# Both directions of a chunked RWKV-7 scan on all four quarters of TensorE

## The reference

```python
h = rms_norm(x, norm_mix);  p = h @ w_in                      # 1024 -> 4832 columns
z = centred_shift(p[..., :RWKV_COLS], mu_prev, mu_next)
y_a = rwkv7_branch(z, ...) @ w_o_rwkv                         # bidirectional recurrence
y_b = conformer_conv_branch(u, ...) @ w_o_conv
x = x + (g_a * y_a + g_b * y_b) @ w_out
x = x + expert_choice_ffn(rms_norm(x, norm_ffn), ...)         # 16 experts
```

```python
def step(S, inp):
    r_t, w_t, k_t, v_t, a_t, b_t = inp
    sa = jnp.einsum('bhij,bhj->bhi', S, a_t)
    S = (S * w_t[:, :, None, :] + sa[..., :, None] * b_t[..., None, :]
         + v_t[..., :, None] * k_t[..., None, :])
    return S, jnp.einsum('bhij,bhj->bhi', S, r_t)
```

## Time and profile before

| | us |
|---|---|
| median of 3 runs | 2510.17 |
| lowest and highest | 2505.96, 2513.14 |
| the profiled execution | 2512.39 |
| its span, first to last instruction | 2510.6 |

### The profile page before, as it was taken

One profiled execution on the slowest core, in us unless ns is written; L12 is line 12 of the kernel. 1 busy time (PEld: TensorE's weight loads), 2 busy tenths in 40 slices (PEclk: granted clock), 3 DMA queues, 4 the chain that ended last, 5 costly groups with the idle time before them and its releaser, 6 DMA issues. The chain is left out here.

```text
span 2510.6 us, 50080 instructions
## 1 busy us (share of the span) xinstructions
PE 2330.4 (93%) x19504; PEld 2038.1 (81%) x19504; DVE 1825.2 (73%) x2480; ACT 1207.5 (48%) x1748; POOL 704.6 (28%) x715
## 2 busy tenths in 40 slices
PE   6899999999986999997989996699999999999997
PEld 4788888888876899986767674699999999999996
DVE  5547888988865576665767677677777777777777
ACT  6355454445522334433335332566555666666656
POOL 2234242433412444455454534001111111101011
PEclk9999999999997999998999998799999999999998
DMA  4335353442537767763647352777777777777777
GB/s 151 85 97 162 86 160 117 135 151 85 173 112 226 210 184 190 193 163 94 235 133 252 105 201 101 301 252 251 268 257 245 237 254 259 248 254 259 263 255 239
DMA packets 294772, 479.74 MB, mean 191 GB/s; under 512 B 142224, under 2 KB 209952, under 8 KB 266832
## 3 DMA queue, kind: packets, MB, share of 16 engines
q1 hardware_dynamic: 275552, 412.52, 50.4%
q0 software_dynamic: 7760, 27.08, 4.9%
q10 hardware_dynamic: 11296, 37.82, 4.6%
HBM read 363.51 MB, written 110.69 MB: 189 GB/s over the span
## 5 line engine op out<-in xcount | busy, mean ns | idle before, releaser
L2749 PE MATMUL bank<-e_xt,e_w_high 128*128 128x384 f32 x1792 | 525.2, 357 | 2.3 <-DVE e_xt L2917 2.3
L2904 DVE TENSOR_TENSOR e_w_low<-e_w,e_w_high 128x2048 fp32r<-128x2048 f32 x192 | 435.9, 2284 | 69.8 <-ACT e_w_high L2805 69.8
L2750 PE MATMUL bank<-e_xt,e_w_low 128*128 128x192 f32 x1792 | 449.3, 251 | 0.0
L2805 ACT ACTIVATE e_w_high<-e_w 128x2048 fp32r<-128x2048 f32 x192 | 366.1, 1908 | 108.0 <-PE bank L2771 79.2
L2750 PEld LDWEIGHTS bank<-e_xt,e_w_low 128*128 128x128 f32 x1792 | 342.5, 191 | 0.6
L2749 PEld LDWEIGHTS bank<-e_xt,e_w_high 128*128 128x128 f32 x1792 | 338.3, 189 | 3.9 <-issue 2.7
L462 PE MATMUL bank<-h_high,w_high 128*128 128x512 f32 x864 | 257.9, 407 | 1.5 <-DVE work L872 1.5
L855 DVE SCALAR_TENSOR_TENSOR work<-work,vec 128x1551 f32<-128x1551 f32 x116 | 243.8, 2102 | 2.4
L465 PE MATMUL bank<-h_low,w_high 128*128 128x512 f32 x864 | 244.8, 391 | 0.0
L468 PE MATMUL bank<-h_high,w_low 128*128 128x512 f32 x864 | 243.7, 390 | 0.0
L2683 POOL DMA_INDIRECT xacc_dram<-e_y,e_put x30 | 47.3, 1576 | 652.0 <-DVE e_y L2939 647.5
(11 more groups left out here) (356 smaller groups left out, 5164.6 us busy)
## 6 DMA issues: line engine op xcount, KB each, us to landing
e_w<-in_ew SPq DMA_DIRECT2D x192, 1024.0 KB, 5.5
features_dram<-work SPq DMA_DIRECT2D x48, 512.0 KB, 3.3
fe<-features_dram SPq DMA_DIRECT2D x24, 1024.0 KB, 8.3
x_w<-in_w_mix SPq DMA_DIRECT2D x48, 512.0 KB, 4.1
w<-in_w_in ACTq DMA_DIRECT2D x35, 512.0 KB, 3.6
ba_tok_dram<-work SPq DMA_DIRECT2D x96, 128.0 KB, 2.2
gates_dram<-work ACTq DMA_DIRECT2D x16, 768.0 KB, 4.6
all<-ba_tok_dram SPq DMA_DIRECT2D x96, 128.0 KB, 3.3
```

The lines of the kernel that those rows point to most:

```text
L2749: nc.tensor.matmul(*wide, start=(k == 0), stop=False)
L2750: nc.tensor.matmul(*narrow, start=False, stop=False)
L2805: nc.scalar.activation(w_high[n % RING][:], w[n % RING][:], ACT.Copy).then_inc(w_high_done, 1)
L2904: tt(w_low[n % RING][:], w[n % RING][:], w_high[n % RING][:].bitcast(F32), ALU.subtract)\
```

## The change

Direction 1 keeps its inputs where they were, but its 64x64 products go to the other half of the partitions: `HALF[d]` gives the output half, `ROWS` for direction 0 and `ROWS[::-1]` for direction 1. So where the two directions' matmuls alternate, four in a row fall on four different quarters. `level_n`, `level_x` and `solve` become one section for both directions; `products` is cut into `products_wide` (128 columns) and `products_narrow` (64), each for both directions, and `products_c` alternates too.

What comes out exchanged is put back: DVE adds the identity for direction 1 in two instructions of 64 partitions, ACT copies `XX` and `GH` of direction 1 in halves, and the copies of level 0 are cut by side for both directions. For direction 1 state and token rows change places (`STATE`, `TOKEN`) and so does the order of B, A, M in `ALL`, with the store of `ba_tok` in `project` to match. The level masks write the blocks that they need, in two instructions, into buffers cleared at the start. `ALL` has six buffers instead of five.

The orders of PE, DVE and ACT are written anew: narrow products behind level_x(0), wide ones behind level_n(1), products_c before level_x(1), and state(1, i-1) moves from the end of `body(i)` to `body(i+1)` behind its first level_n. SP's and POOL's orders stay; SP's store of G waits for the wide mask alone.

```diff
-        ALL = many("all", [P, HP, 5, CH], RING)
-        B_, A_, M_, G_, RB_ = range(5)
+        ALL = many("all", [P, HP, 5, CH], RING_ALL)
+        B_, A_, M_, G_, RB_ = (0, 2), (1, 1), (2, 0), (3, 3), (4, 4)
+        STATE, TOKEN = ROWS, ROWS[::-1]
+        HALF = [ROWS, ROWS[::-1]]
...
+                    x = XX if n else X0
                     for hp in L4:
-                        for r in ROWS:
-                            mm = nc.tensor.matmul(t_bank(d)[r, hp, :], NL[d][s][r, n, hp, :], x[d][s][r, hp, 0, :],
-                                                  start=True, stop=True)
-                    mm.then_inc(m_n[d], 1)
+                        for d in DIRS:
+                            for z, r in enumerate(ROWS):
+                                mm = nc.tensor.matmul(t_bank(d)[HALF[d][z], hp, :], NL[d][s][r, n, hp, :],
+                                                      x[d][s][r, hp, 0, :], start=True, stop=True)
+                            if hp == HP - 1:
+                                mm.then_inc(m_n[d], 1)
...
                 def body(i):
                     post, pre = i >= 1, i + AHEAD < NCH
-                    for d in DIRS:
-                        level_n(d, i, 0)
+                    level_n(i, 0)
+                    if i >= 2:
+                        state(1, i - 2)
                     if post:
-                        for d in DIRS:
-                            solve(d, i - 1)
-                    for d in DIRS:
-                        level_x(d, i, 0)
+                        solve(i - 1)
+                    level_x(i, 0)
+                    if pre:
+                        products_narrow(i + AHEAD)
                     if post:
                         full(0, i - 1)
+                    level_n(i, 1)
                     if pre:
-                        products(0, i + AHEAD)
-                    for d in DIRS:
-                        level_n(d, i, 1)
+                        products_wide(i + AHEAD)
                     if post:
                         full(1, i - 1)
                     if pre:
-                        products(1, i + AHEAD)
-                    for d in DIRS:
-                        level_x(d, i, 1)
+                        products_c(i + AHEAD)
+                    level_x(i, 1)
                     if post:
                         state(0, i - 1)
-                    if pre:
-                        products_c(i + AHEAD)
-                    if post:
-                        state(1, i - 1)
...
-                    copy(GH[d][:].rearrange("p h c -> p (h c)"), bank[EARLY[d]][:]).then_inc(a_g[d], 1)
+                    for out, src in swapped(d):
+                        ins = copy(GH[d][out, :, :].rearrange("p h c -> p (h c)"), bank[EARLY[d]][src, :])
+                    ins.then_inc(a_g[d], 1)
...
-                def level_n(d, i, n):
-                    dve.wait_ge(m_n[d], i * LEVELS + (n + 1))
-                    if n >= 1 or i >= 1:
-                        dve.wait_ge(m_x[d], i * LEVELS + n)
-                    tt(T1[d][:], t_bank(d), ident, ALU.add).then_inc(v_t[d], 1)
+                def level_n(i, n):
+                    for d in DIRS:
+                        dve.wait_ge(m_n[d], i * LEVELS + (n + 1))
+                        if n >= 1 or i >= 1:
+                            dve.wait_ge(m_x[d], i * LEVELS + n)
+                    tt(T1[0][:], t_bank(0), ident(P), ALU.add).then_inc(v_t[0], 1)
+                    for out, src in zip(ROWS, ROWS[::-1]):
+                        ins = tt(T1[1][out, :, :], t_bank(1)[src, :, :], ident(HD, src), ALU.add)
+                    ins.then_inc(v_t[1], 1)
```

More of the change, by code:

```diff
@@ L1273, in level_x @@
-                    mm.then_inc(m_x[d], 1)
-                def solve(d, i):
-                    pe.wait_ge(a_x[d], i * LEVELS + LEVELS)
-                    landed(pe, l_t, d, i, 32)
-                    if d == 0:
-                        ahead = min(i + 1 + AHEAD, NCH)
-                        pe.wait_ge(v_c[0], ahead)
-                        pe.wait_ge(v_c[1], ahead)
-                    for hp in L4:
-                        for r in ROWS:
-                            mm = nc.tensor.matmul(bank[EARLY[d]][r, hp * P:(hp + 1) * P], XX[d][i % 2][r, hp, d, :],
-                                                  ALL[d][i % RING][r, hp, B_:RB_ + 1:RB_ - B_, :], start=True, stop=True)
-                    mm.then_inc(m_g[d], 1)
+                        for y in range(2) if n < LEVELS - 1 else (None,):
+                            for d in DIRS:
+                                side = d if y is None else y
+                                for z, r in enumerate(ROWS):
+                                    pair = (x[d][s][r, hp, 1, :], T1[d][r, hp, :])
+                                    left, right = pair if side == 0 else pair[::-1]
+                                    mm = nc.tensor.matmul(x_bank(d)[HALF[d][z], hp, side, :], left, right,
+                                                          start=True, stop=True)
+                                if hp == HP - 1 and y != 0:
+                                    mm.then_inc(m_x[d], 1)
@@ L1403, in _ @@
                 for j in range(AHEAD):
-                    for d in DIRS:
-                        products(d, j)
+                    products_wide(j)
+                    products_narrow(j)
                     products_c(j)
@@ L1486, in _ @@
                 for i in range(NCH):
+                    if i >= 2:
+                        out(1, i - 2)
+                        store(1, i - 2)
                     if i >= 1:
@@ L1508, in _ @@
                         root()
+                out(1, NCH - 2)
+                store(1, NCH - 2)
                 for d in DIRS:
@@ L1685, in conv @@
                     if i == 6:
[L1686 removed]
+                        dve.wait_ge(c_read, 1)
                         for k in range(CT):
```

343 lines of the change are left out of this document (194 added, 149 removed).

## The result

| | before | after |
|---|---|---|
| median of 15 runs | 2507.67 us | 2517.92 us |
| lowest and highest | 2503.81, 2516.44 | 2509.64, 2526.16 |
| ratio after/before, 95% interval | | 1.0038 [1.0027, 1.0049] |
| the profiled execution | 2512.39 | 2519.17 |

The change is slower by about 10 us. The prediction said 8 us faster: the sign is wrong. That the time still lies inside its range (2486 to 2518), by 0.1 us, is luck.

What follows compares the result with a forecast made beforehand. PE (15.0 us a step) bounds, with POOL's and SP's 31.9 us two-step round nearly as long behind it. Eight rounds at 31.2 give about -6, the end -2.5, together -8.4: 2504 us (2502 against the median), range 2486 to 2518.

Steps and rivals of the forecast that it cites:

- PE's part: PE's sections in a chunk step: 10.4 us of them halved by four quarters, a step from 15.0 to 9.8 us.
- the round through POOL: POOL's and SP's work over two chunk steps, inversion included: 31.9 us a round, 16.0 a step, before the change.
- the closed round: Moved state makes SP's value load, and so POOL's next round, wait for the last round's expansion: 31.2 us a round.
- rival 3: Closed round with lower clock and long DMA legs or a stretched inversion: 33.3 us a round, total 2520; chance 20%.
- All this is hidden if the round of rows 3 is longer than two steps: Added DVE and ACT work per step (DVE to 11.6 us, ACT 2 to 3 more) hides behind POOL's two-step round.
- in front of every second level_n, ended by POOL's expansion: Sign of being right: PE idles 5 to 8 us there in the regular part, about 65% busy.
- Its own sign for this: Sign of being wrong: PE's waits for DVE's adds longer than those for POOL.
- the moved state: state(1, i-1) behind the next level_n: SP's value load waits for it; level product, state and hand-overs take 3.4 us.
- The path through POOL: POOL and SP over two steps as one chain, with the 12.0 us inversion in it, nearly as long as PE's steps.
- The halves on DVE and ACT: Split T1 add and copies: DVE 0.4 to 0.9 us a step more, ACT 2 to 3, hidden behind the round.
- The clearing of buffers: Clearing the level buffers at the start, before the first features land: 0 us, bounds -1 to +2.
- The overhead of a matmul: By the skill's 60-cycle rule, 64-column sections would shrink to about 0.8 us, not 0.5; 2.4 us more in all.

Runs made afterwards that it cites:

- e14: The kernel before with its feature products issued as fewer, wider matmuls over head pair 0 (36 fewer a step, all heads get those products); ratio to before 0.9976.
- e3: The kernel before with 7 of 14 row steps of POOL's inversion left out, that part of the inverse not computed; ratio to before 0.9965.
- e1: The change with state(1, i-1), its copy and its carry put back at the end of step i; ratio to before 1.0043.
- e17: The change with direction 1's outputs on their own half (mostly two quarters) and its copies and T1 add whole; ratio to before 1.0079.
- e2: The change with 7 of 14 row steps of POOL's inversion left out, that part of the inverse not computed; ratio to before 1.0019.
- e6: The change with feature loads from the fifth on cut to 64 of 2048 columns, a third of the scan's DMA bytes; ratio to before 1.0015.
- e19: The change with both level masks early and level_n, level_x and solve issued direction 0 first, then direction 1, instead of alternating; ratio to before 1.0020.
- e18: The kernel before with direction 1's T1 add and GH and XX copies in halves, level 0 copies cut by side; ratio to before 1.0019.
- e5: The change with DVE's level masks of direction 1 moved from the step's end to directly behind those of direction 0; ratio to before 1.0021.
- e16: The change with both level masks early and direction 1's sum fu in front of the second wide mask on DVE; ratio to before 1.0043.
- e4: The change with direction 1's outputs left on their own half, same instructions and order but mostly two quarters instead of four; ratio to before 1.0073.

## Why the prediction was wrong

- **PE's part** was right in kind: the regular part lost 51 us of PE time where 5.2 us a step are 73. The step's terms were close at the full clock (level products 0.63 and 0.51 for the 0.5, but the wide ones 1.03 for the 0.9). The time at the lower clock (30.7 against 6.6 us in the stretch) takes back some 12 us. The clock was 0.93; "near 0.9" was forecast.
- **The bound before the change** was misread. PE's own step of 15.0 us is right, but the other 1 us of the mean step was put down to the round through POOL, and the forecast's -6 us was that round made shorter. Of the 15 steps from chunk 4 to chunk 19 seven take 14.95 to 14.97 us. The other eight hold what makes the mean 15.96: PE's idle time (7.9 us, most of it the pauses with no releaser), two stretches at the lower clock behind a wait (6.8 us, which cost half of that), and an extra section in two of them (1.1 us each). None of them holds a wait for POOL. e14 took work and pauses from PE and the step fell to 15.41; e3 took 5 us from the inversion and it hardly moved (15.84).
- **The forecast's size of the closed round** was close: 32.6 against 31.25. From the end of the value load to the even expansion it was 28.1 us on average (27.2 forecast), from there to the next load 4.5 (4.05). A number near rival 3's, 2520, could be read as its proof. e1 shows that it isn't: without the closed round the time is the same.
- **The step that failed** is "All this is hidden if the round of rows 3 is longer than two steps", with the idle time that was to stand "in front of every second level_n, ended by POOL's expansion". The prediction set PE's work of 9.8 us and the round of 31 us against each other, and left out the third thing: the chain of hand-overs within a step, PE to DVE or ACT and back, in which DVE and ACT got nothing shorter. In its place the runs showed 57 us of idle time in 224, none of it ended by POOL: waits for DVE's level masks (9.4) and sums (8.4), pages of instructions (23.7 inside sections) and waits with no releaser. Its own sign for this, waits of PE for DVE longer than those for POOL, is what the profile shows, though for masks and sums and not for the adds that it named. The reordering of PE, DVE and ACT, for which it had no term but the moved state, costs 20 us (e17), and the moved state isn't it (e1); the quarters were worth 9, not the 100 us of PE time that they were to save in 20 steps. That the chain is as long as before, for the reason given, is an argument; no run measures it.
- **The start of the scan** was not in the sum: the merged first section waits 3.4 us longer for the second feature load, 1 us of which stays until chunk 4.
- **The path through POOL** was read as one chain with the inversion in it. e2 shows that the inversion has company in SP's queue. As a path that is nearly as long as the step it was read rightly: e6 and e19 run into it.
- **The halves on DVE and ACT** as hidden: right within the 1 to 9 us of e18. The clearing of buffers, forecast at 0: the four clearings on DVE end before the first matmul and it does not wait for them.
- **The overhead of a matmul.** The prediction weighed what the Trainium skill says in TensorEngine Tiling (Array Packing), section Instruction Overhead, and had 0.8 us for a level product by it. 0.63 and 0.51 were measured.

Not settled: which part of the new order costs the 20 us. The place of state(1) (e1) and the level masks' place (e5, e16) bring nothing clear of noise when they are changed alone, each on four quarters and with the other waits in place; e19 leaves the merging of the level sections open. Left besides are the merging of the product sections and their places on PE, the places of their masks on DVE, and the waits for both directions at once. No run separates what the lower clock costs in the total: in the whole scan (750 to 1185 us) it was granted for 112 us in after, 53 in before and 44 in e17, so it is no part of e17's 20 us, but it may have eaten part of what the quarters gave. And what holds the regular step at 16.0 us in nearly all of these kernels on four quarters: the runs exclude the inversion, the instruction count and the feature bytes each by itself, and leave the PE-DVE-ACT chain, SP's queue and POOL's round behind it, which may well take turns. No kernel tried is faster than before with all its computation in it.

## What to carry to other kernels

When an engine is busy 97% and its work is cut by a third, look for what takes a step with that engine at zero: write down the chain of hand-overs between engines once around the step, with the other engines' durations, before any saving is counted. Where a step is longer than an engine's own work, find the microseconds in the trace before a second path is made responsible for them. A reordering is a change of its own and wants its own term; measured nearly alone (here on two quarters) it can cost more than what it makes room for brings. A forecast mechanism whose number fits is not confirmed by that; the run that takes it away decides. And a run that takes one wait away and gains little hasn't cleared that wait while others of the same length stand behind it.

## What the runs showed of the hardware

- PE's instructions arrive in pages of 16 KB, some 250 of its records. Where PE uses them up in short matmuls at 16 to 20 ns a record on four quarters, it pauses at the end of half of the pages (22 of 43, inside sections) for 0.3 to 3.5 us, and goes on about 1.45 us after the page's packet has ended. With two quarters (31 ns; before, e4, e17) there are 2.3 to 6.4 us of such pauses in 224, with four in after 23.7.
- A float32 matmul with 128 weight columns and 64 moving columns costs about 125 ns a record (2.00 us for 16), two on 128x64 tiles side by side together 69 ns (1.10 us for 32 records). The weight loads' records are longer too, 192 against 138 ns; that they are the cause isn't shown.
- 64x64 tiles with 64 columns take 20 ns a record on four quarters at the first level product (0.63 us for 32) and 16 at the second (0.51), against 31 on two (0.98).
- The same columns in fewer, wider matmuls are a little shorter on PE: 0.86 us for 0.90 (4 records of 512 columns for 16 of 128, e14).
- A DMA issued from ACT's queue costs ACT 0.6 us, as on SP, and that is time in which its next copy doesn't start.
